# Seven-product gate units: another order of work on ScalarE and VectorE, two homes for the first weight sum, the second plain gate held for the next chunk, the gap's modulation weights in free space

## The reference, cut to what matters

```python
h2 = _rmsnorm(x, norm2_g[l]) * (1 + sc2) + sh2                       # (tokens, 1024)
a, b = jnp.split(_dwconv3(h2 @ w_up[l], ffn_conv_w[l]), 2, axis=-1)  # D_FF = 2816 each
x = x + g2 * ((jax.nn.silu(a) * b) @ w_down[l])
```

## Time and profile before

| what | value |
|---|---|
| time, median of 3 runs | 1715.43 us (1714.87 to 1717.39) |
| time of the profiled execution | 1713.49 us |
| its span, first to last instruction | 1711.7 us |
| mean granted TensorE clock | 0.973 |
| TensorE matmuls | 1600.2 us busy, 93% of the span, 10563 |
| VectorE / ScalarE | 1061.9 us (62%) / 739.1 us (43%) |
| DMA traffic | 236.13 MB, mean 138 GB/s |

### The profile page before, as it was taken

One profiled execution on the slowest core, in us unless ns is written; L12 is line 12 of the kernel. 1 busy time (PEld: TensorE's weight loads), 2 busy tenths in 40 slices (PEclk: granted clock), 3 DMA queues, 4 the chain that ended last, 5 costly groups with the idle time before them and its releaser, 6 DMA issues. The chain is left out here.

```text
span 1711.7 us, 26600 instructions
## 1 busy us (share of the span) xinstructions
PE 1600.2 (93%) x10563; PEld 1479.9 (86%) x10563; DVE 1061.9 (62%) x1778; ACT 739.1 (43%) x1275; POOL 143.4 (8%) x172
## 2 busy tenths in 40 slices
PE   5999999998899999999989999999889989999998
PEld 4677888987799999999977788889779989989998
DVE  4773666636764765756768547675577467466573
ACT  3543444326543543524444444442555245253352
POOL 0000000000201201112000000000021121120210
PEclk7899999999999999999989999999899999999999
DMA  9455011372856846758425531113175685584762
GB/s 327 152 179 179 25 50 37 111 248 82 187 138 154 197 130 161 172 136 188 132 87 171 180 106 50 50 38 112 52 189 135 156 189 135 150 192 121 186 155 77
DMA packets 284235, 236.13 MB, mean 138 GB/s; under 512 B 10640, under 2 KB 254928, under 8 KB 284112
## 3 DMA queue, kind: packets, MB, share of 16 engines
q1 hardware_dynamic: 259584, 189.82, 35.6%
q0 software_dynamic: 23680, 44.05, 14.6%
q10 hardware_dynamic: 848, 0.56, 0.1%
HBM read 188.78 MB, written 3.67 MB: 112 GB/s over the span
## 5 line engine op out<-in xcount | busy, mean ns | idle before, releaser
L953 PE MATMUL ps<-hc_hi,w_hi 128*128 128x322 f32 x1120 | 358.0, 320 | 55.2 <-ACT u L1389 32.7
L955 PE MATMUL ps<-hc_lo,w_hi 128*128 128x322 f32 x1120 | 353.4, 316 | 0.0
L957 PE MATMUL ps<-hc_hi,w_lo 128*128 128x322 f32 x1120 | 352.7, 315 | 0.0
L1895 DVE TENSOR_TENSOR w_lo<-raw,w_hi 128x1024 fp32r<-128x1024 f32 (+1 forms) x160 | 174.2, 1089 | 176.1 <-ACT w_hi L1370 176.0
L953 PEld LDWEIGHTS ps<-hc_hi,w_hi 128*128 128x128 f32 x1120 | 215.6, 193 | 68.0 <-ACT u L1389 39.4
L1370 ACT ACTIVATE w_hi<-raw 128x1024 fp32r<-128x1024 f32 x120 | 126.5, 1059 | 321.0 <-DMA raw<-raw 145.9
L548 POOL DMA_DIRECT2D raw<-raw x160 | 138.6, 922 | 1200.1 <-DMA raw<-in_w_up_dram 940.5
L1010 PE MATMUL ps<-gg,w_hi 128*128 128x322 f32 x704 | 219.2, 311 | 0.7 <-DVE gg L1887 0.7
L1011 PE MATMUL ps<-gg,w_hi 128*128 128x322 f32 x704 | 218.9, 311 | 0.0
L1012 PE MATMUL ps<-gg,w_lo 128*128 128x322 f32 x704 | 218.4, 310 | 0.0
L955 PEld LDWEIGHTS ps<-hc_lo,w_hi 128*128 128x128 f32 x1120 | 215.7, 193 | 0.0
(11 more groups left out here) (194 smaller groups left out, 2876.7 us busy)
## 6 DMA issues: line engine op xcount, KB each, us to landing
raw<-in_w_up_dram SPq DMA_DIRECT2D x280, 256.0 KB, 3.6
raw<-raw POOLq DMA_DIRECT2D x160, 256.0 KB, 3.8
raw<-in_w_mod_dram SPq DMA_DIRECT2D x72, 512.0 KB, 4.5
raw<-in_w_in_dram SPq DMA_DIRECT2D x48, 512.0 KB, 4.7
raw<-in_w_down_dram SPq DMA_DIRECT2D x16, 768.0 KB, 4.4
raw<-in_w_down_dram SPq DMA_DIRECT2D x16, 640.0 KB, 4.1
raw<-in_w_out_dram SPq DMA_DIRECT2D x16, 512.0 KB, 4.3
pre_w<-in_w_mod_dram SPq DMA_DIRECT2D x8, 512.0 KB, 10.1
```

Source lines behind the costliest of these rows:

```text
L953: mm(out, whi_f[:, c0:c0 + P], hc_hi[:, k, part, :], start=first and k == 0, stop=False, skip_group_check=not first)
L955: mm(out, whi_f[:, c0:c0 + P], hc_lo[:, k, part, :], start=False, stop=False, skip_group_check=not first)
L957: ins = mm(out, wlo_f[:, c0:c0 + P], hc_hi[:, k, part, :], start=False, stop=k == KH - 1, skip_group_check=not first)
L1895: V.tensor_tensor(wlo_f[:, c0:c1], raw_f[:, r0:r0 + c1 - c0], whi_f[:, c0:c1].bitcast(F32), ALU.subtract).then_inc(up_lo[i], 1)
```

## The change

The numbers of matmuls, splits and DMAs of the seven-product units stay the same. The plain gates are now 0 and 6, both still computed at the start of the layer; gate 6's result is copied to a buffer of its own, `ub_held`, and it goes through taps, `silu` and `gate_mult` during the first chunk's down phase. The chunks hold 5 seven-product units each. The first sum is made in block 1 or in a new block 8 by turns (`s1_block`), its load waits for the unit before the last, and GpSimd makes it for the next gate right after the last sum of this one. SyncE, ScalarE and VectorE get another order of work. The weights of pair `GAP_A[l]` go to `mod_t`, loaded ahead of `split[14]`, and no longer through the ring; ScalarE takes the modulation row before the second plain gate's split, and makes `hfull` first and the high part from it by one `Copy`. VectorE's split of that gate moves forward to tile 5. `dve.drain()` between taps is replaced by waits on VectorE's own semaphores.

```diff
-N_GATE, N_CLASSIC = FF // P, 2
+N_GATE = FF // P
+CLASSIC = [0, 6]
-MOD_RING = MOD_LAYER - 2
+MOD_RING = MOD_LAYER - 4
-        return order + split[14:17] + mod[12:14] + split[17:18]
+        return order + split[14:18]
...
-    return order + mod[18:22] + split[17:18]
+    return order + mod[18:20] + split[17:18]
...
+def s1_block(g):
+    return (8, 1)[(g - s_gates(chunk_of(g))[0]) % 2]
...  SyncE
+                    if (kind, n) == ("split", O_U + 2):
+                        sp.wait_ge(o_read, ROUNDS * (l + 1))
+                        for i in range(2):
+                            layer, unit = mod_source(2 * GAP_A[l] + i)
+                            sp.dma_start(mod_t[:, i, :]..., w_mod_v[...]).then_inc(modt_full, 16)
...
                     block(a22_block(g), 1, 1, g)
+                    if i >= 2:
+                        sp.wait_ge(up_lo[0], n - 1)
+                        sp.wait_ge(sum_full[2], 16 * (n - 1))
...
+                    block(s1_block(g), 1, 0, g)
                     if i:
                         sp.wait_ge(up_lo[0], n)
-                        sp.wait_ge(sum_full[2], summed(l, g - 1))
-                        sp.wait_ge(sum_full[4], summed(l, g - 1))
+                        sp.wait_ge(sum_full[4], 16 * n)
...
                     block(0, 0, 0, g)
-                    block(1, 1, 0, g)
...  GpSimd
+                first_sum(FIRST)
+                for g in S_GATES:
                     pool.wait_ge(sum_full[1], summed(l, g))
                     pool.wait_ge(blk_full[2], loaded(l, g, 2))
-                    add_block(2, 1)
+                    add_block(2, s1_block(g), 2)
...
+                    add_block(5, 2, 5)
+                    if g != S_GATES[-1]:
+                        first_sum(S_GATES[S_GATES.index(g) + 1])
...  ScalarE, gap
+                rows(l, GAP_A[l])
                 split_hi(G_U + 1)
-                rows(l, GAP_A[l])
...
+                h_full(0)
+                h_high(0)
+                h_full(1)
+                for k in range(1, KT):
+                    if k < KT - 1:
+                        h_full(k + 1)
+                    h_high(k)
...  ScalarE, one unit
-                        if prev is not None:
-                            if prev < N_CLASSIC:
-                                gate_copy(prev)
-                            else:
-                                c21(prev)
-                            centre(prev, 0)
-                        up_split_hi(g, 3)
-                        snapshot(g, s1, bx, 1, c11_ready, s1_ready)
-                        if prev is not None:
-                            centre(prev, 1)
...
+                        elif prev is not None:
+                            c21(prev)
+                            centre(prev, 1)
+                        snapshot(g, s1, bx, 1, c11_ready, s1_ready)
+                        if g == FIRST:
+                            combo_hi(T4, 1, 0, 4)
                         up_split_hi(g, 3)
+                        snapshot(g, p5, by, 2, c22_ready, p5_ready)
+                        if prev is not None and prev != HELD:
+                            silu(prev)
                         if nxt is not None:
                             up_split_hi(nxt, 0)
-                        snapshot(g, p5, by, 2, c22_ready, p5_ready)
                         snapshot(g, u2, bx, 3, c12_ready, u2_ready)
...
                         if prev is not None:
                             gate_hi(prev)
                         if nxt is not None:
+                            up_split_hi(nxt, 1)
                             up_split_hi(nxt, 2)
+                        else:
+                            down_split_hi(c, 0)
+                        centre(g, 0)
...  VectorE
-                split_lo(G_U + 1)
+                    if i == 5:
+                        split_lo(G_U + 1)
...
+                            first_taps(prev)
+                            last_taps(prev)
+                        if g == FIRST:
+                            combo_lo(T4, h21, 4)
+                        up_split_lo(g, 3)
+                        if prev is not None and prev != HELD:
+                            gate_mult(prev)
+                        if nxt is not None:
+                            up_split_lo(nxt, 0)
                         c11(g)
+                        if prev is not None:
+                            gate_lo(prev)
+                        c22(g)
                         if nxt is not None:
                             up_split_lo(nxt, 1)
+                            c12(g)
+                            up_split_lo(nxt, 2)
...
                     down_add(c, 0)
+                    if last + 1 == HELD:
+                        first_taps(HELD)
+                        last_taps(HELD)
                     down_split_lo(c, 2)
```

More of the change, by code:

```diff
@@ L116, in s_gates @@
 def s_gates(c):
-    return range(max(CH0[c], N_CLASSIC), CH0[c] + CHUNKS[c])
+    return [g for g in range(CH0[c], CH0[c] + CHUNKS[c]) if g not in CLASSIC]
 def bank_set(g):
@@ L136, in a22_block @@
     return 7 - (g - s_gates(chunk_of(g))[0]) % 2
+def s1_block(g):
+    return (8, 1)[(g - s_gates(chunk_of(g))[0]) % 2]
+S_GATES = [g for g in range(N_GATE) if g not in CLASSIC]
 def su(l, g):
-    return S_LAYER * l + g - N_CLASSIC
+    return S_LAYER * l + S_GATES.index(g)
 def loaded(l, g, b):
-    if b >= 6:
-        return 16 * (sum(a22_block(j) == b for j in range(N_CLASSIC, N_GATE)) * l
-                     + sum(a22_block(j) == b for j in range(N_CLASSIC, g + 1)))
+    if b >= 6 or b == 1:
+        return 16 * (sum(b in (a22_block(j), s1_block(j)) for j in S_GATES) * l
+                     + sum(b in (a22_block(j), s1_block(j)) for j in S_GATES if j <= g))
     return 16 * (su(l, g) + 1)
@@ L203, in hybrid_step @@
         x = sb("x", [P, KT, T])
-        raw = sb("raw", [P, 2, SLOT])
+        raw_all = sb("raw_all", [P, 9 * BLK])
         early = ExitStack()
@@ L454, in _, with free_of_slot0 @@
                     else:
-                        gate_unit(n % 2, n - G_U)
+                        gate_unit(n % 2, CLASSIC[n - G_U])
+                def free_of_slot0():
+                    before, j = ORDER[l][-2]
+                    free_of_split(j) if before == "split" else free_of_mod(j + 1)
                 def block(b, row, half, g):
@@ L915, in _ @@
                 for u in range(2):
[L916 to L917 removed]
+                    mod_sum(l, GAP_A[l], u, "t", None)
                 spread(l, 2)
@@ L1441, in _ @@
                     gate_hi(last)
+                    if last + 1 == HELD:
+                        centre(HELD, 0)
+                        centre(HELD, 1)
                     down_split_hi(c, 2)
+                    if last + 1 == HELD:
+                        silu(HELD)
                     if c < len(CHUNKS) - 1:
                         down_split_hi(c, 3)
-                        up_split_hi(CH0[c + 1], 0)
-                        up_split_hi(CH0[c + 1], 1)
+                        up_split_hi(s_gates(c + 1)[0], 0)
+                        up_split_hi(s_gates(c + 1)[0], 1)
                     elif l < LAST:
@@ L1985, in _ @@
+                        c22(g)
                         if nxt is not None:
                             up_split_lo(nxt, 1)
+                            c12(g)
+                            up_split_lo(nxt, 2)
                         else:
                             down_split_lo(c, 0)
-                        c22(g)
-                        if prev is not None:
-                            gate_lo(prev)
-                        c12(g)
-                        if nxt is not None:
-                            up_split_lo(nxt, 2)
@@ L1995, in _ @@
-                    last = CH0[c] + CHUNKS[c] - 1
-                    centred(last, 0)
-                    taps(last, 0, 0)
-                    centred(last, 1)
-                    taps(last, 1, 0)
-                    dve.drain()
-                    taps(last, 0, 2).then_inc(taps_ready, 1)
-                    taps(last, 1, 2).then_inc(taps_ready, 1)
+                            c12(g)
+                    last = CH0[c] + CHUNKS[c] - 1
+                    first_taps(last)
+                    last_taps(last)
@@ L2018, in _ @@
                     down_add(c, 2)
+                    if last + 1 == HELD:
+                        gate_mult(HELD)
                     down_split_lo(c, 3)
```

237 lines of the change are left out of this document (119 added, 118 removed).

## The result

The changed kernel takes 1639.89 us (median of four runs, 1638.46 to 1643.47), the kernel before 1715.2 beside it. The ratio is 0.9561, 95% interval 0.9543 to 0.958: 75 us less. The forecast moved the kernel by 57 us; the profiled spans moved by 70.1 (1711.7 to 1641.6).

The account below looks back on a forecast made before the run. TensorE was taken as the bound, busy 1600.2 of 1711.7 us, so only idle time and clock could be won. Terms -46.6 (stretches) - 7.0 - 5.0 (gap stage) + 1.6 (modulation weights) = -57.0 gave 1658 us, range 1640 to 1688.

Parts of the forecast that it names:

- The old ring of 14.1 us: Seven-product units: first sum waits for sum 4 through block 0's load; one turn 14.1 us where TensorE needs 12.5.
- rings (a) and (b): Transfer rings in the seven-product units, turns 10.9 to 12.5 and 10.5 to 11.8 us; loss 2.5 us per stretch, 20 in all.
- that spends the 1.5: Chunk's first unit: sum 5 at 12.4 uses up the 1.5 us it may be late before product 2 waits.
- ring (a): Seven-product units: sum 5 lands, blocks 2 and 3 load, sum 2, sum 5 again; 10.9 to 12.5 us a turn.
- Rival C: Seven-product units: late sum 5 holds up ScalarE, and TensorE at product 2; slower above 1.83 + 0.26 us per unit; 1732; chance 0.05.
- Table load: First unit of each layer: `silu`'s 1.28 us table load inside the unit makes product 4 wait 1.5 to 1.8, 3.6 us in all.
- Clock: Seven-product stretches: lowered TensorE clock after waits of 1.5 to 2 us costs 3 us, less than before.
- `c22` and ScalarE's order: Seven-product units: `c22` ahead of VectorE's low split removes product 6's 0.8 us waits, 15.2 us; ScalarE's `p5` comes ahead of its split.
- The held gate: Gate 6's taps and product in the down phase: cost nothing; without cover at most 3.5 us per layer.
- Gap stage: Earlier tile start on ScalarE and no wait ahead of product 0: -7.0 us in layer 0, -5.0 in layer 1.
- `mod_t`: Layer 0: modulation weights loaded ahead of `split[14]` delay the next sums, +1.6 us, bounds 0 and 5; layer 1: 0.
- Rival A: Seven-product units: the DMA engines are the bound, transfers collide and rings stretch, 36 us loss instead of 20; 1676; chance 0.22.

Follow-up runs that it names:

- changed, again: The changed kernel, unaltered, run once more on another chip beside three variants: 1639.62 us, ratio 0.9553 to the kernel before.
- load of the first sum's block late: Changed kernel with the load of the first sum's block again behind block 0 and the wait for sum 4, both homes kept: 1694.14 us, ratio 0.9885.
- one home: Changed kernel with only block 1 for the first sum, its load waiting for the previous unit's split and second sum: 1659.82 us, ratio 0.9681.
- ScalarE's old order: Changed kernel with, on ScalarE, the split of the next unit's blocks 0 and 1 ahead of `p5` and `silu` behind `u2`: 1638.88 us, ratio 0.9565.
- VectorE's old order: Changed kernel with, on VectorE, the low split of blocks 2 and 3 ahead of `c22` and `gate_lo` behind it: 1643.6 us, ratio 0.9583.
- both old orders: Changed kernel with the old mid-unit order on both ScalarE and VectorE, first sum's place and two homes kept: 1645.69 us, ratio 0.9632.
- more traffic: Changed kernel with one more unread 256 KB load in each seven-product unit of three chunks a layer: 1644.52 us, ratio 0.9617.
- the kernel without the held gate: Changed kernel with plain gates 0 and 1 both worked off in the first chunk, chunks of 4, 6, 5 and 5 units: 1645.75 us, ratio 0.9629.
- the two old places: Changed kernel with ScalarE's split of unit 17 ahead of the modulation row and VectorE's low split of it behind all `h` tiles: 1645.87 us, ratio 0.959.

## Why the prediction missed, step by step

**Where the stretches lose.** In a stretch without waits a matmul starts 0.1485 us after the one before. The lists of waits show less than a late start costs: they leave out idle times up to 0.15 us and count from the modelled end of the matmul before, some 0.16 us behind the next regular start. So here is what the starts of the matmuls lose over 0.1485 us, summed over the 40 units and put down to the product whose start is late:

| kernel | product 2 (`s`) | product 4 (`u`) | product 6 (`c22`) | all else | sum, us |
|---|---|---|---|---|---|
| before | 2.3 | 39.5 | 20.3 | 11.2 | 73.3 |
| changed | 7.2 | 2.7 | 0.0 | 1.1 | 11.0 |
| changed, again | 2.1 | 2.7 | 0.0 | 1.4 | 6.2 |
| load of the first sum's block late | 12.2 | 39.9 | 0.1 | 7.5 | 59.7 |
| one home | 23.4 | 4.9 | 0.0 | 2.1 | 30.4 |
| ScalarE's old order | 2.4 | 0.2 | 2.4 | 1.4 | 6.4 |
| VectorE's old order | 2.3 | 2.7 | 6.2 | 1.0 | 12.2 |
| both old orders | 0.7 | 0.2 | 14.3 | 0.2 | 15.4 |
| more traffic | 10.6 | 2.7 | 0.0 | 2.7 | 16.0 |

**What bounds the kernel, and the first sum: right.** The old ring of 14.1 us was what held the units; putting one load back restores it (54 of the 75 us, and the 39.9 us ahead of product 4). The second home is a part of it that I had not priced by itself: 20 us, nearly all of it ahead of product 2.

**The other rings: the step that failed, by its size.** I gave rings (a) and (b) 2.5 us in each of eight stretches, 20 us: sum 5 was to come at 12.4 in a chunk's first unit, "that spends the 1.5", and the next three turns were to cost 0.8 each. What stands in its place is the loss ahead of product 2 and the little behind it: 7 us in this trace and 2 in the second trace of the same kernel. Here are GpSimd and ScalarE in the second stretch, which starts at 539.52. GpSimd's order is sum 2, sum 4, sum 5 and then the next gate's first sum; the rows are sums 4 and 5 (545.48), then sum 2 (556.01), sum 5 (559.93), sum 2 (567.97) and sum 5 (572.33, 585.80) of the next gates:

```profile
545.48 1.75 POOL L587 DMA_DIRECT2D raw_all<-raw_all  x2 [7.53 <-DMA raw_all<-in_w_up_dram]
...
556.01 0.85 POOL L587 DMA_DIRECT2D raw_all<-raw_all  x1 [6.30 <-DMA raw_all<-in_w_up_dram]
...
559.93 0.85 POOL L587 DMA_DIRECT2D raw_all<-raw_all  x1 [1.51 <-DMA raw_all<-raw_all]
...
567.97 0.85 POOL L587 DMA_DIRECT2D raw_all<-raw_all  x1 [5.06 <-DMA raw_all<-in_w_up_dram]
...
572.33 0.85 POOL L587 DMA_DIRECT2D raw_all<-raw_all  x1 [1.49 <-DMA raw_all<-raw_all]
...
585.80 0.85 POOL L587 DMA_DIRECT2D raw_all<-raw_all  x1 [1.13 <-DMA raw_all<-raw_all]
```

```profile
551.03 1.06 ACT L1441 ACTIVATE w_hi<-raw_all 128x1024 fp32r<-128x1024 f32 x1 [3.09 <-DMA raw_all<-raw_all]
...
564.14 1.06 ACT L1441 ACTIVATE w_hi<-raw_all 128x1024 fp32r<-128x1024 f32 x1 [3.37 <-DMA raw_all<-raw_all]
...
577.48 1.06 ACT L1441 ACTIVATE w_hi<-raw_all 128x1024 fp32r<-128x1024 f32 x1 [4.30 <-DMA raw_all<-raw_all]
...
589.08 1.06 ACT L1441 ACTIVATE w_hi<-raw_all 128x1024 fp32r<-128x1024 f32 x1 [2.42 <-DMA raw_all<-raw_all]
```

ScalarE's split starts when sum 5 has landed. The first time that is 11.5 us after the unit's start and not 12.4: blocks 4 and 5 have been loaded at 6.0 where I had 7.7, and from there the two issues and the landing take 5.5 us where I had 4.65. From then on ring (a) sets the time, since sum 5 waits each time for the landing of sum 2: the load of blocks 2 and 3 takes 5.0 us (551.03 to 556.01), sum 2 3.9, sum 5 4.2, together 13.1; the next turn is 3.8, 4.4 and 5.1, together 13.3. I had 10.9 to 12.5. So the split comes later in the unit, 11.5, 12.1, 12.9 us after its start. From the start of the split to the end of the snapshot `s` ScalarE has 3.4 us of work (551.03 to 554.47), and product 2 is due at 12.5 + 3.6, so TensorE begins to wait when the split starts later than about 12.6: in the fourth unit, by 0.3 us. The last turn takes 11.6 us, and the split is back at 12.0. In all eight stretches of both traces the last turn is the shortest (10.8 to 12.5 us; the turns ahead of it take 12.6 to 15.3). The worst is one of 15.3 us in the stretch of 645.16, where sum 2 waited for sum 1 as with one home: 1.9 us in its fourth unit.

So I had the chain right, the turn too short and the start 0.9 too late. The 0.8 us of drift did not follow from my rings, whose slowest turn of 12.5 is as long as a unit; that 0.6 and 0.8 were measured is luck. And the drift does not go on to the end of a stretch: a sixth unit does not make it much worse (1.5 and 1.1 us in the stretches of six units of the kernel without the held gate). Rival C's path through `s` is thus real, and its price stays far below the 1.83 us per unit from which it would decide.

**Table load: a little less, then nothing.** TensorE waited 1.0 us twice and not 1.8 (2.7 us in the table above, where I had 3.6), and its removal gave nothing. ScalarE in the first unit:

```profile
437.51 1.28 ACT L1404 ACT_TABLE_LOAD   x1
438.81 0.74 ACT L1404 ACTIVATE tmp<-tmp 128x644 f32<-128x644 f32 x1
```

The next instruction starts 1.30 us after the load did, 1.29 in the earlier trace rows; the 1.38 us of drain that the Trainium skill's page "ScalarE: Activation LUTs" (section "What ACT_TABLE_LOAD costs") adds are not in this trace either.

**Clock: none.** I took 3 us; the granted clock is 1.00 in all eight windows. Together the stretches gave 62.3 us instead of 46.6, the bulk of the miss. Of these 15.7 us 13 are loss that I had given to the rings and that did not come, 3 the clock, 1 the table load, less the 1 that the matmuls lose without a wait.

**`c22` and ScalarE's order.** I added the 15.2 us for `c22` to the gain of the first sum and put them down to VectorE's order. It takes both orders: with both back product 6 loses 14.3 us, with VectorE's alone 6.2, with ScalarE's alone 2.4 (in the two first units). And they are not a gain of their own size. A unit with the late `c22` takes some 12.8 us, nearer to the turn of ring (a), and what product 6 loses is then not lost ahead of product 2 (0.7 us instead of 7.2 or 2.1) and product 4. So both back cost 4 to 9 us in the stretches, 5 to 12 by the times, and not 15.

**The held gate: a gain where I had none.** I had priced only what it costs. It gains 6 to 12 us by the times. In the profiled stretches, 511.96 us without it, it is 2 to 7; the first stretches alone lose 9.3 us without it and 4.3 or 3.0 with it. Since the edit also moves gate 0's `silu`, the share of each was not tried.

**Gap stage: right in sum, in part by luck.** `stat(2)` to the first tile fell by 3.0 us in layer 0 and 3.3 in layer 1 (from 15.6 to 12.3), first tile to first unit by 3.6 and 3.0: 6.6 and 6.3 where I had 7.0 and 5.0. The wait for the modulation row is gone from the tiles' start. But `stat(2)` to the first tile differs between kernels whose gap stage is the same, 10.3, 11.9 or 13.5 us in layer 0 and 10.7 or 12.3 in layer 1, with the clock: the `mod_t` sum behind `stat(2)` takes 1.93 us in the short cases and 2.4 to 3.6 in the others. The kernel before had the short sum in layer 0 and the long one (3.15) in layer 1. So one trace tells this gain only to 1.6 us a layer, or 3.2 in layer 0. By the experiment with the two old places their gain is not ahead of the first unit at all (1.9 us less there with the old ones in each layer) but in the first stretch, 5.8 and 5.3 us.

**`mod_t`: right place, price too low.** Forecast +1.6, bounds 0 and 5; measured +6.1, outside them. I counted the late landing at TensorE's next sums and left out two things. VectorE's `mod_post(6)` stands behind `split_lo(14)`, whose weights are late as well, so TensorE waits for `modv` (3.33 us) and not for a load. And 5.7 us at a granted clock of 0.50 follow, where a product of twelve matmuls takes 3.2 us and not 1.8.

**The sum.** -62.3 - 6.6 - 6.3 + 6.1 - 1.8 in the down phases + 0.8 in the stages with no change give -70.1, as the profiled spans do. The profiled execution is 3.6 us above its median, before it was 1.7 below, hence the 75.3 between the medians. Of the 18 us by which the median missed the forecast, 13 are between the profiled executions: 15.7 from the stretches, less the 4.5 of `mod_t`, and small sums. The other 5 are which execution was profiled.

**Rival A** had a true premise (share 1.00 in a unit) and a false conclusion. The Trainium skill's rule of turns between queues ("DMA: Bandwidth & Descriptors", "Queues, rings and completion order") fits what is seen of the sums: sum 5 lands 3.2 us after its issue at 585.80, where the DMA share until then is 0.73, and 5.0 after its issue at 572.33, where it is 0.97. No run here separates that rule from other causes. But 0.2 to 0.3 us a load is all that more traffic costs, in a stretch whose engines are busy 0.82 with it and 0.79 without.

**Still open.** What sets the length of one turn between 12.6 and 15.3 us, and why the last one is shorter, is not shown. No step below some 5 us can be told from one trace: two traces of the same kernel differ by 5 us in the stretches.

## What to carry to other kernels

A ring that is a little longer than the stage it feeds costs nothing until its drift has used up the slack. Reckon start, slack, drift per turn and the number of turns, and take the turn's length from the whole chain at the load it will have. Tell like transfers apart by their order in the program and by what each waits for: the rows of GpSimd's four sums look the same, and how a timeline groups them changes from unit to unit. When a load is put ahead of others in a queue, follow each thing that it makes late through the in-order engines, not only to its own reader. Waits of one engine with different names may share one cause, and taking away one can bring out the other: price them together, and sum the starts, since a list of waits hides many small ones.

## What the hardware showed that was not expected

- The DMA engines were busy 1.00 of a unit at 227 GB/s and TensorE lost nothing; in other windows they moved 309 GB/s at 0.91. A share near 1.00 did not mean that no more could be moved: one more load of 256 KB per unit cost 0.2 to 0.3 us.
- After 3.33 us without work TensorE ran at a granted clock of 0.50 for the next 5.7 us. Behind the plain gates' waits of 1.43 and 1.63 us (400.38 and 410.70) the windows show 1.00.
- In layer 0, after a wait of 0.55 us ahead of `ones` times `sq` and its ten matmuls of one column, the `mod_t` sum took 3.20 us at a granted clock of 0.58. The same wait and the same matmuls stand ahead of it in the kernel with `mod_t` loaded earlier and in the kernel before, and there the sum took 1.93 us. So the same sequence has either clock behind it, and what decides is not shown.
- A sum of 256 KB inside SBUF landed between 3.1 and 6.4 us after its issue, 4.1 in the median, in one execution.
